# Low halves of the last three down chunks: a ScalarE negation and an accumulating transfer from GpSimd in place of a VectorE subtraction

## The chip, the cores and the metric

The kernel runs on one core of one Trainium2 chip. The metric is the device time of one execution in microseconds. Its engines are TensorE (PE, with weight loads as PEld), VectorE (DVE), ScalarE (ACT), GpSimd (POOL) and SyncE (SP), which issues most of the transfers. SBUF is the core's working memory.

## The reference

Two transformer blocks over 512 tokens of width 1024, in f32: a gated MLP layer with spatial mixing, a shared key/value projection with a dilated attention layer, and a second block of two attentions and a feed-forward layer. The change touches only the very end, the down projection of that feed-forward layer, with D_FF = 2816 = 22 x 128:

```python
h2 = _modulate(x, ln2_g[l], sh2, sc2)
y = (jax.nn.silu(h2 @ w_gate[l]) * (h2 @ w_up[l])) @ w_down[l]
x = x + g2[:, None, :] * y
```

## The kernel before

All weights stream through the core as 108 chunks of 128 rows, numbered w, in one fixed order. Every engine runs a program of its own, written out by hand, and they meet at semaphores.

To reach f32 accuracy, each chunk is split into two fp32r tiles: `w_hi` holds the rounded weights, `w_lo` the rest. The activations are split likewise, and each product is made of three matmuls: hi by hi, hi by lo, lo by hi. So a chunk passes through four steps:

- SP's `load` (L388) brings it from HBM to `w_raw[par]`, with par = w % 2. It waits until `lo_done` says that the low half of chunk w-2 is made, since that was the last reader of the raw buffer.
- ACT's `to_hi` (L575) copies `w_raw` to `w_hi`. It waits for the load and, by `mm_done`, for the matmuls of chunk w-2, which read the same `w_hi` and `w_lo`.
- DVE's `to_lo` (L1009) writes `w_lo = w_raw - w_hi` and counts `lo_done`.
- PE waits in `chunk_ready` (L1808) for `lo_done` and runs the matmuls (L1775).

There are two buffers of each tile, so chunk w is split while PE works on chunk w-1.

The down projection is done in two parts. The first 16 of the 22 row tiles (`FF1`) are handled earlier. The last six (`FF2`) come in chunks w = 104 to 107 (`W_DN2` to `W_END - 1`). Each of these has 6 x 256 = 1536 columns and gives two output tiles of 128 rows, 18 matmuls of 512 columns each, 36 in a chunk. Ahead of them come the gate and up chunks, up to w = 103. The split of chunk 104 is made inside that loop (`gate_up`, the call of `to_hi` and `to_lo` with `next_chunk`), so that only the chunks 105, 106 and 107 have their split in the code at the end. In program order, ACT's last gate work (`gu_hi`, L977) stands ahead of its `to_hi` of chunk 105.

After each output tile DVE's `update_x` (L1001) adds the gated result from PSUM to `x`, and SP sends that tile of `x` out (L507). These stores stand on SP's queue behind the four last loads. The PSUM tile that chunk w writes was freed by the `update_x` of chunk w-2.

Of the kernel before, what the change touches and what calls it, by code (L numbers as in the profile page):

```python
# [21 lines left out]
F32 = mybir.dt.float32  # L22
F32R = mybir.dt.float32r
ACT = mybir.ActivationFunctionType
# [16 lines left out]
FF1, FF2 = 16, 6  # L41
# [15 lines left out]
W_DN2 = W_GU2 + FF2  # L57
W_END = W_DN2 + 4
# [51 lines left out]
def program(nc, d):  # L110
# [4 lines left out]
    def at(name, shape, off, dt=F32):  # L115
        return nc.alloc_sbuf_tensor_at(name, shape, dt, offset=off)

    def take(nbytes, step=64):
        off = top[0]
        top[0] += (nbytes + step - 1) // step * step  # L120
        return off
# [10 lines left out]
    w_raw = [at(f"w_raw{s}", [P, 2048], take(8 * KB)) for s in range(2)]  # L132
# [13 lines left out]
    w_hi = [at(f"w_hi{s}", [P, 2048], off_whi[s], F32R) for s in range(2)]  # L146
    w_lo = [at(f"w_lo{s}", [P, 2048], off_wlo[s], F32R) for s in range(2)]
# [130 lines left out]
    def sem(name):  # L278
        return nc.alloc_semaphore(name)
# [4 lines left out]
    w_loaded = [sem("w_loaded0"), sem("w_loaded1")]  # L284
# [8 lines left out]
    hi_done, lo_done, lo_half_done = sem("hi_done"), sem("lo_done"), sem("lo_half_done")  # L293
# [24 lines left out]
    qk2_done, s2_freed, max2_part, exp2_done = sem("qk2_done"), sem("s2_freed"), sem("max2_part"), sem("exp2_done")  # L318
    inv2_done, p2_ready, turn2_done, pt2_done, pv2_done = sem("inv2_done"), sem("p2_ready"), sem("turn2_done"), sem("pt2_done"), sem("pv2_done")
    mhi_done, mlo_done, diff_freed = sem("mhi_done"), sem("mlo_done"), sem("diff_freed")  # L320
    tanhg_done, gz_done, guhi_done, gulo_done = sem("tanhg_done"), sem("gz_done"), sem("guhi_done"), sem("gulo_done")


# [16 lines left out]
    def ge(eng, semaphore, value):  # L340

        if not isinstance(value, int) or value > 0:
            eng.wait_ge(semaphore, value)
# [3 lines left out]
    def weights_at(u, par):  # L347

        if isinstance(u, int) and 2 * u + par in V_CHUNKS:
            return wv_hi[par], wv_lo[par]  # L350
        return w_hi[par], w_lo[par]
# [24 lines left out]
    with block:  # L376
# [3 lines left out]
        def _(sp):  # L380
            weights, ada_weights = d["weights"], d["ada"]

            def load(u, par, used=2048):

                src = weights[bass.ds(2 * u + par, 1), :, 0:used].rearrange("a p n -> p (a n)")
                sp.lower_ap_dma(src)
                ge(sp, lo_done, 2 * u + par - 3)
                sp.dma_start(w_raw[par][:, 0:used], src).then_inc(w_loaded[par], 16)  # L388
# [111 lines left out]
                for par in range(2):  # L500
                    load(u, par)
            for w in range(W_DN2, W_END):
                load(*divmod(w, 2), FF2 * 256)

            for m in range(KT):
                sp.wait_ge(acc_freed, 2 * W_DN2 - 15 + m)
# [4 lines left out]
        @block.gpsimd  # L511
        def _(pool):
            def stage(j, par):

                ge(pool, mix_done, j - 1)
                nc.gpsimd.tensor_tensor(v_stage[par][:, :, :], v[:, :, bass.ds(j * P, P)],
                                        v_stat[:, 5, :].unsqueeze(2).broadcast_to([P, TB, P]), ALU.mult).then_inc(v_staged, 1)

            def sum_squares(k, total, tile):

                for m in range(1, KT - 1):
                    pool.wait_ge(sq_ready, 8 * k + m + 1)
                    if m > 1:
                        pool.wait_ge(sq_added, 6 * k + m - 1)
                    nc.gpsimd.tensor_tensor(total, tile(0) if m == 1 else total, tile(m), ALU.add).then_inc(sq_added, 1)

            nc.gpsimd.memset(one_row[:, :], 1.0).then_inc(one_ready, 1)
            nc.gpsimd.memset(idle[:, :].bitcast(F32), 0.0).then_inc(idle_ready, 1)
            nc.gpsimd.memset(half_r[:, :].bitcast(F32), 0.0).then_inc(half_zeroed, 1)
            nc.gpsimd.memset(eps_tile[:, :], EPS)  # L530
            nc.gpsimd.memset(ones_r[:, :].bitcast(F32), 1.0).then_inc(ones_ready, 1)
            pool.wait_ge(half_zeroed, 1)
            pool.wait_ge(ones_ready, 1)
            for e in range(2):
                if e:
                    pool.wait_ge(half_ready, 1)
                part = slice(64 * e, 64 * e + 64)
                nc.gpsimd.memset(half_r[part, part].bitcast(F32), 1.0).then_inc(half_ready, 1)
            pool.wait_ge(half_ready, 2)
            pool.wait_ge(v_stat_dve, 3)  # L540
            stage(0, 0)
            stage(1, 1)
            with pool.Fori(1, AT // 2) as i:
                for par in range(2):
                    stage(2 * i + par, par)

            sum_squares(1, sq_sum[:, :], lambda m: sq_a[m % 2][:, :])

            def quarters(m):

                pool.wait_ge(exp_done, 4 * m + 4)
                ge(pool, spread_done, m)
                stats = row_stat[:, 0, :, :].rearrange("p k n -> p (k n)").unsqueeze(1).broadcast_to([P, 4, 16])
                nc.gpsimd.tensor_tensor(row_apart[:, :, :], stats, own_quarter.unsqueeze(2).broadcast_to([P, 4, 16]), ALU.mult).then_inc(apart_done, 1)

            pool.wait_ge(blocks_loaded, 16)
            for m in range(QH):
                quarters(m)
            pool.wait_ge(pv_done, 4 * QH)
            nc.gpsimd.memset(wf_hi[:, :, :].bitcast(F32), 0.0).then_inc(wf_zeroed, 1)  # L560
            nc.gpsimd.memset(wf_lo[:, :, :].bitcast(F32), 0.0).then_inc(wf_zeroed, 1)
            sum_squares(2, sq_sum[:, :], lambda m: sq[m % 2][:, :])
            sum_squares(3, sq_sum[:, :], lambda m: sq[m % 2][:, :])


        @block.scalar
        def _(act):
            eps_col = eps_tile[:, :]

            def to_hi(u, par, used=2048):  # L570

                act.wait_ge(w_loaded[par], 16 * u)
                if not (isinstance(u, int) and 2 * u + par == 2):
                    act.wait_ge(mm_done, 4 * u + 2 * par - 2)
                nc.scalar.activation(weights_at(u, par)[0][:, 0:used], w_raw[par][:, 0:used], ACT.Copy).then_inc(hi_done, 1)  # L575
# [411 lines left out]
            with act.Fori(W_GU2 // 2, W_DN2 // 2) as u:  # L987
                for par in range(2):
                    gate_up(u, 2 * (u - W_GU2 // 2) + par, par, FF1)

            for w in range(W_DN2 + 1, W_END):
                to_hi(*divmod(w, 2), FF2 * 256)


        @block.vector
        def _(dve):
            def f32(tile):
                return tile.bitcast(F32)
# [4 lines left out]
            def to_lo(u, par, used=2048):  # L1003

                dve.wait_ge(hi_done, 2 * u + par - 1)

                ge(dve, lo_done, 2 * u + par - 2)
                hi, lo = weights_at(u, par)
                nc.vector.tensor_tensor(lo[:, 0:used], w_raw[par][:, 0:used], f32(hi[:, 0:used]), ALU.subtract).then_inc(lo_done, 1)  # L1009
# [143 lines left out]
            def update_x(m, acc, gate, mm, n, dilate=False):  # L1153

                dve.wait_ge(mm_done, mm)
                xm = dilated(x[:, m, :]) if dilate else x[:, m, :]
                stt(xm, four(acc) if dilate else acc, mods[:, bass.ds(m + gate, 1)], xm, ALU.mult, ALU.add).then_inc(acc_freed, n)
# [357 lines left out]
            for c in range(4):  # L1515
                w = W_OUTB + c
# [190 lines left out]
            for c in range(4):  # L1707
                w = W_OUT2 + c
# [54 lines left out]
                    gate_up(u, 2 * (u - W_GU2 // 2) + par, par, FF1)  # L1763
            for c in range(4):
                w = W_DN2 + c
                if c < 3:
                    to_lo(*divmod(w + 1, 2), FF2 * 256)
                for half in range(2):
                    update_x(2 * c + half, G[2 * (w % 2) + half][:, :], GATE_2, 2 * w + half + 1, 1)

# [2 lines left out]
        def _(pe):  # L1773
# [34 lines left out]
            def chunk_ready(u, par):  # L1808
                pe.wait_ge(lo_done, 2 * u + par - 1)
# [157 lines left out]
            for c in range(NKV // 2):  # L1967
                w = W_KV + 2 * c
# [296 lines left out]
            for t in range(1, 5):  # L2265
# [3 lines left out]
                for u in range(12):  # L2269
# [15 lines left out]
                    if project:  # L2285
                        mi, w = u // 2, w0 + u // 4
# [75 lines left out]
            with pe.Fori(W_GU2 // 2, W_DN2 // 2) as u:  # L2362
                gate_up(u)
            for w in range(W_DN2, W_END):
                chunk_ready(*divmod(w, 2))
                for half in range(2):
                    pe.wait_ge(acc_freed, 2 * w + half - 19)
                for piece in (range(FF2 - 2), range(FF2 - 2, FF2)) if w == W_DN2 else (range(FF2),):
                    if w == W_DN2:

                        pe.wait_ge(gulo_done, FF1 + piece[-1] + 1)
                    for half in range(2):
                        last = columns(G[2 * (w % 2) + half][:, :], w % 2, half, FF2, gu_hi, gu_lo_of, piece)
                        if piece[-1] == FF2 - 1:
                            last.then_inc(mm_done, 1)
# [89 lines left out]
```

## Time and profile before

| | |
|---|---|
| time, median of 3 runs (lowest, highest) | 1402.61 us (1402.58, 1405.28) |
| time of the profiled execution | 1403.06 us |
| its span in the profile | 1401.0 us |
| PE busy | 1387.4 us, 99% |
| DVE busy | 963.5 us, 69% |
| ACT busy | 646.1 us, 46% |
| POOL busy | 50.9 us, 4% |
| granted TensorE clock over the span | 1.0 of full speed |

The span is what the profiler saw between the first and the last instruction. The time of the execution is 2.06 us longer. PE's busy time includes the drain of pipelined matmuls, so that its share does not say how near its peak it is; the starts of its instructions do. Chunks 104 to 107 fill about the last 36 us.

### The profile page before, as it was taken

Reading aid. Unit: us, or ns where it says so; the run is one execution under the profiler, and the core shown is the slowest. Engines: PE = TensorE matmul, PEld = TensorE weight load, DVE = VectorE, ACT = ScalarE, POOL = GpSimd, SP = SyncE. Lnnn points to the kernel's source line nnn. Section 1 sums busy time; section 2 is a strip of 40 time slices with the busy share of each in tenths; the row PEclk is TensorE's granted clock in tenths of the full one; section 3 lists DMA queues with packets and bytes.
Section 4 is the critical chain, followed back from the end, with each engine's and each line's share of the span. In section 5 each row is a group of like instructions: output and inputs, shape, how many; then the busy total and the mean of one; then the engine's idle time right before and its main releaser. Section 6 shows DMA issues by size and latency. Waiting matters only on the chain.

```text
span 1401.0 us, 19731 instructions
## 1 busy us (share of the span) xinstructions
PE 1387.4 (99%) x7274; PEld 1158.0 (83%) x7274; DVE 963.5 (69%) x1573; ACT 646.1 (46%) x1046; POOL 50.9 (4%) x55
## 2 busy tenths in 40 slices
PE   8999999999999999999999999999999999999999
PEld 6998888888888888888888777777788888888887
DVE  6976777777898688888887777778775433332333
ACT  4744222333366566666654656666644222211221
POOL 0001000001100000000002000000020000000000
PEclk9999999999999999999999999999999999999999
DMA  9994554457723211112212221111122222222222
GB/s 374 376 394 182 180 179 176 178 203 284 304 76 124 82 69 61 61 61 66 84 60 91 82 100 61 61 61 61 61 91 90 90 102 108 90 90 101 103 74 83
DMA packets 35329, 181.23 MB, mean 129 GB/s; under 512 B 4153, under 2 KB 4921, under 8 KB 20930
## 3 DMA queue, kind: packets, MB, share of 16 engines
q1 hardware_dynamic: 34050, 177.95, 34.5%
q10 hardware_dynamic: 1216, 2.44, 0.5%
q8 instruction: 39, 0.64, 0.2%
q14 instruction: 24, 0.20, 0.0%
HBM read 177.74 MB, written 2.11 MB: 128 GB/s over the span
## 4 chain that ended last, share of the span: by engine, by line
PE 89%; DVE 6%; ACT 2%; DMA 1%; issue 1%; SPq 0%; ACTq 0%; DVEq 0%
PE acc L1775 80%; PE ada L1775 3%; PE norm L1775 2%; PE turn L1775 2%; DMA ada_up<-in_ada_first 1%; PE turn L2069 1%; PE turn L2212 1%; DVE hx L1001 1%; DVE w_lo L1009 1%; DVE s L1574 0%; DVE hk_lo L1001 0%; DVE h_lo L1001 0%; DVE v L1638 0%; ACT hk_hi L599 0%; DVE c_masked L1580 0%
## 5 line engine op out<-in xcount | busy, mean ns | idle before, releaser
L1775 PE MATMUL acc<-h_hi,w_hi 128*128 128x512 f32 x984 | 390.1, 396 | 0.0
L1775 PE MATMUL acc<-h_hi,w_lo 128*128 128x512 f32 x984 | 384.3, 391 | 0.0
L1775 PE MATMUL acc<-h_lo,w_hi 128*128 128x512 f32 x984 | 383.6, 390 | 0.0
L1009 DVE TENSOR_TENSOR w_lo<-w_raw,w_hi 128x2048 fp32r<-128x2048 f32 (+1 forms) x92 | 212.8, 2313 | 58.7 <-ACT w_hi L575 58.6
L575 ACT ACTIVATE w_hi<-w_raw 128x2048 fp32r<-128x2048 f32 (+1 forms) x93 | 176.0, 1892 | 111.4 <-PE acc L1775 111.3
L1775 PEld LDWEIGHTS acc<-h_hi,w_lo 128*128 128x128 f32 x984 | 184.8, 188 | 39.4
L1775 PEld LDWEIGHTS acc<-h_hi,w_hi 128*128 128x128 f32 x984 | 185.2, 188 | 38.2 <-issue 1.2
L1775 PEld LDWEIGHTS acc<-h_lo,w_hi 128*128 128x128 f32 x984 | 185.1, 188 | 36.7
L1775 PE MATMUL acc<-wv_hi,h_hi 128*128 128x256 f32 x320 | 89.6, 281 | 0.0
L1001 DVE SCALAR_TENSOR_TENSOR x<-acc,mods,x 128x512 f32<-128x512 f32 (+1 forms) x40 | 32.9, 827 | 81.6 <-PE acc L1775 81.6
L1775 PE MATMUL acc<-wv_lo,h_hi 128*128 128x256 f32 x320 | 88.2, 277 | 0.0
L1775 PE MATMUL acc<-wv_hi,h_lo 128*128 128x256 f32 x320 | 87.5, 277 | 0.0
L581 ACT ACTIVATE y<-norm,eps_tile 128x512 f32<-128x512 f32 x54 | 37.2, 689 | 77.2 <-PE norm L1775 75.7
L1001 DVE SCALAR_TENSOR_TENSOR gu<-tanh_g,acc 128x512 f32<-128x512 f32 x21 | 14.4, 688 | 82.5 <-PE acc L1775 82.4
L1775 PE MATMUL acc<-gu_lo,w_hi 128*128 128x512 f32 x176 | 68.5, 389 | 0.0
L1775 PE MATMUL acc<-gu_hi,w_hi 128*128 128x512 f32 x176 | 68.5, 389 | 0.0
L1775 PE MATMUL acc<-gu_hi,w_lo 128*128 128x512 f32 x176 | 68.5, 389 | 0.0
L977 ACT ACTIVATE gu_hi<-gu 128x512 f32 (+1 forms) x22 | 13.9, 632 | 117.2 <-DVE gu L1001 117.2
L1775 PEld LDWEIGHTS acc<-wv_hi,h_hi 128*128 128x128 f32 x320 | 60.2, 188 | 1.2 <-issue 1.0
L1775 PEld LDWEIGHTS acc<-wv_lo,h_hi 128*128 128x128 f32 x320 | 60.1, 188 | 0.2
L1775 PEld LDWEIGHTS acc<-wv_hi,h_lo 128*128 128x128 f32 x320 | 59.6, 188 | 0.0
L1001 DVE SCALAR_TENSOR_TENSOR ada_out<-ada_out,csil 128x1024 f32<-128x1024 f32 x32 | 38.4, 1224 | 17.3 <-DMA ada_out<-in_ada 17.0
(306 smaller groups left out, 2528.2 us busy)
## 6 DMA issues: line engine op xcount, KB each, us to landing
w_raw<-in_weights SPq DMA_DIRECT2D x102, 1024.0 KB, 4.8
ada_v<-in_ada SPq DMA_DIRECT2D x32, 512.0 KB, 6.3
ada_raw<-in_ada SPq DMA_DIRECT2D x32, 512.0 KB, 5.8
ada_out<-in_ada SPq DMA_DIRECT2D x32, 512.0 KB, 6.3
ada_up<-in_ada_first SPq DMA_DIRECT2D x8, 1024.0 KB, 17.3
w_raw<-in_weights SPq DMA_DIRECT2D x4, 768.0 KB, 4.1
x<-in_x SPq DMA_DIRECT2D x2, 1024.0 KB, 6.0
w_first<-in_weights SPq DMA_DIRECT2D x4, 512.0 KB, 13.7
```

The source lines that it names most:

```text
L575: nc.scalar.activation(weights_at(u, par)[0][:, 0:used], w_raw[par][:, 0:used], ACT.Copy).then_inc(hi_done, 1)
L581: nc.scalar.activation(y0[:, :], total, ACT.Ln, scale=1.0 / count, bias=eps_col).then_inc(ln_done, 1)
L977: nc.scalar.activation(gu_hi[:, f, :], gu[par][:, :], ACT.Copy).then_inc(guhi_done, 1)
L1001: return nc.vector.scalar_tensor_tensor(out, in0, scalar, in1, op0, op1, **more)
L1009: nc.vector.tensor_tensor(lo[:, 0:used], w_raw[par][:, 0:used], f32(hi[:, 0:used]), ALU.subtract).then_inc(lo_done, 1)
L1775: return nc.tensor.matmul(out, lhsT, rhs, start=start, stop=stop)
L2069: turned = nc.tensor.transpose((T0, T1)[c % 2][:, P * b:P * b + P], s_b[tile][:, lo:lo + P], ident)
L2212: turned = nc.tensor.transpose(T0[:, P * b:P * b + P], s_2[n % 3][:, 0, P * b:P * b + P], ident)
```

## The change

For the chunks 105, 106 and 107, DVE no longer makes `w_lo`. Instead

- ACT, right after `to_hi`, waits for its own result (`hi_done`) and writes `w_lo = -w_hi` with a second activation, counting `neg_done`;
- GpSimd waits for `neg_done` and issues a transfer from `w_raw` to `w_lo` with `accum_op=add`: for each element the transfer adds what it read from `w_raw` to what stands in `w_lo`. Its end is counted by `rest_added[par]`;
- PE waits for `rest_added` instead of `lo_done` ahead of the chunks 105 to 107;
- SP's load of chunk 107 overwrites the raw buffer of chunk 105, so it waits for `rest_added[1]` of chunk 105 instead of `lo_done`.

The values computed are the same. GpSimd issues no transfer anywhere in the kernel before.

```diff
--- before.py
+++ after.py
@@ -318,6 +318,7 @@
     qk2_done, s2_freed, max2_part, exp2_done = sem("qk2_done"), sem("s2_freed"), sem("max2_part"), sem("exp2_done")
     inv2_done, p2_ready, turn2_done, pt2_done, pv2_done = sem("inv2_done"), sem("p2_ready"), sem("turn2_done"), sem("pt2_done"), sem("pv2_done")
     mhi_done, mlo_done, diff_freed = sem("mhi_done"), sem("mlo_done"), sem("diff_freed")
+    neg_done, rest_added = sem("neg_done"), [sem("rest_added0"), sem("rest_added1")]
     tanhg_done, gz_done, guhi_done, gulo_done = sem("tanhg_done"), sem("gz_done"), sem("guhi_done"), sem("gulo_done")
 
 
@@ -500,7 +501,10 @@
                 for par in range(2):
                     load(u, par)
             for w in range(W_DN2, W_END):
-                load(*divmod(w, 2), FF2 * 256)
+                if w < W_END - 1:
+                    load(*divmod(w, 2), FF2 * 256)
+            sp.wait_ge(rest_added[1], 16)
+            sp.dma_start(w_raw[1][:, 0:FF2 * 256], weights[W_END - 1][:, 0:FF2 * 256]).then_inc(w_loaded[1], 16)
 
             for m in range(KT):
                 sp.wait_ge(acc_freed, 2 * W_DN2 - 15 + m)
@@ -561,6 +565,11 @@
             nc.gpsimd.memset(wf_lo[:, :, :].bitcast(F32), 0.0).then_inc(wf_zeroed, 1)
             sum_squares(2, sq_sum[:, :], lambda m: sq[m % 2][:, :])
             sum_squares(3, sq_sum[:, :], lambda m: sq[m % 2][:, :])
+
+            used = FF2 * 256
+            for w in range(W_DN2 + 1, W_END):
+                pool.wait_ge(neg_done, w - W_DN2)
+                pool.dma_start(w_lo[w % 2][:, 0:used].bitcast(F32), w_raw[w % 2][:, 0:used], accum_op=ALU.add).then_inc(rest_added[w % 2], 16)
 
 
         @block.scalar
@@ -988,8 +997,11 @@
                 for par in range(2):
                     gate_up(u, 2 * (u - W_GU2 // 2) + par, par, FF1)
 
+            used = FF2 * 256
             for w in range(W_DN2 + 1, W_END):
-                to_hi(*divmod(w, 2), FF2 * 256)
+                to_hi(*divmod(w, 2), used)
+                act.wait_ge(hi_done, w - 1)
+                nc.scalar.activation(w_lo[w % 2][:, 0:used], w_hi[w % 2][:, 0:used].bitcast(F32), ACT.Copy, scale=-1.0).then_inc(neg_done, 1)
 
 
         @block.vector
@@ -1763,8 +1775,6 @@
                     gate_up(u, 2 * (u - W_GU2 // 2) + par, par, FF1)
             for c in range(4):
                 w = W_DN2 + c
-                if c < 3:
-                    to_lo(*divmod(w + 1, 2), FF2 * 256)
                 for half in range(2):
                     update_x(2 * c + half, G[2 * (w % 2) + half][:, :], GATE_2, 2 * w + half + 1, 1)
 
@@ -2362,7 +2372,10 @@
             with pe.Fori(W_GU2 // 2, W_DN2 // 2) as u:
                 gate_up(u)
             for w in range(W_DN2, W_END):
-                chunk_ready(*divmod(w, 2))
+                if w == W_DN2:
+                    chunk_ready(*divmod(w, 2))
+                else:
+                    pe.wait_ge(rest_added[w % 2], 32 if w == W_END - 1 else 16)
                 for half in range(2):
                     pe.wait_ge(acc_freed, 2 * w + half - 19)
                 for piece in (range(FF2 - 2), range(FF2 - 2, FF2)) if w == W_DN2 else (range(FF2),):
```

The end of ACT's program, after the last gate work; `w_hi_62` and `w_lo_64` are the tiles of the odd chunks (105, 107), `w_hi_61` and `w_lo_63` those of chunk 106. Before:

```order
L987 REGISTER_ALU
L987 COMPARE_AND_BRANCH
L575 ACTIVATE w_hi_62<-w_raw_53 128x1536 [waits mm_done,w_loaded1]
L575 ACTIVATE w_hi_61<-w_raw_52 128x1536 [waits mm_done,w_loaded0]
L575 ACTIVATE w_hi_62<-w_raw_53 128x1536 [waits mm_done,w_loaded1]
L376 UNCONDITIONAL_BRANCH
```

And now:

```order
L996 REGISTER_ALU
L996 COMPARE_AND_BRANCH
L584 ACTIVATE w_hi_62<-w_raw_53 128x1536 [waits mm_done,w_loaded1]
L1004 ACTIVATE w_lo_64<-w_hi_62 128x1536 [waits hi_done]
L584 ACTIVATE w_hi_61<-w_raw_52 128x1536 [waits mm_done,w_loaded0]
L1004 ACTIVATE w_lo_63<-w_hi_61 128x1536 [waits hi_done]
L584 ACTIVATE w_hi_62<-w_raw_53 128x1536 [waits mm_done,w_loaded1]
L1004 ACTIVATE w_lo_64<-w_hi_62 128x1536 [waits hi_done]
L377 UNCONDITIONAL_BRANCH
```

Behind each copy to `w_hi` stands a second activation of the same size, which waits for the copy ahead of it.

The end of SP's queue: the loads of the chunks 104 to 107 and the stores. Before:

```order
L388 DMA w_raw_52<-in_weights 128x1536 [waits lo_done]
L388 DMA w_raw_53<-in_weights 128x1536 [waits lo_done]
L388 DMA w_raw_52<-in_weights 128x1536 [waits lo_done]
L388 DMA w_raw_53<-in_weights 128x1536 [waits lo_done]
L507 DMA out<-x 128x512 [waits acc_freed] x8
L376 UNCONDITIONAL_BRANCH [waits stored]
```

And now:

```order
L389 DMA w_raw_52<-in_weights 128x1536 [waits lo_done]
L389 DMA w_raw_53<-in_weights 128x1536 [waits lo_done]
L389 DMA w_raw_52<-in_weights 128x1536 [waits lo_done]
L507 DMA w_raw_53<-in_weights 128x1536 [waits rest_added1]
L511 DMA out<-x 128x512 [waits acc_freed] x8
L377 UNCONDITIONAL_BRANCH [waits stored]
```

The order is the same; the fourth load, with the eight stores behind it, waits for a transfer from GpSimd to land instead of for VectorE.

The end of GpSimd's program. Before:

```order
L525 TENSOR_TENSOR sq_sum<-sq_sum,sq_94 128x512 [waits sq_added,sq_ready]
L525 TENSOR_TENSOR sq_sum<-sq_sum,sq_93 128x512 [waits sq_added,sq_ready]
L525 TENSOR_TENSOR sq_sum<-sq_sum,sq_94 128x512 [waits sq_added,sq_ready]
L525 TENSOR_TENSOR sq_sum<-sq_sum,sq_93 128x512 [waits sq_added,sq_ready]
L376 UNCONDITIONAL_BRANCH
```

And now:

```order
L529 TENSOR_TENSOR sq_sum<-sq_sum,sq_94 128x512 [waits sq_added,sq_ready]
L529 TENSOR_TENSOR sq_sum<-sq_sum,sq_93 128x512 [waits sq_added,sq_ready]
L572 DMA w_lo_64<-w_raw_53 128x1536 [waits neg_done]
L572 DMA w_lo_63<-w_raw_52 128x1536 [waits neg_done]
L572 DMA w_lo_64<-w_raw_53 128x1536 [waits neg_done]
L377 UNCONDITIONAL_BRANCH
```

Three accumulating transfers have come in behind GpSimd's last additions, in the order of the chunks 105, 106, 107.

## Rows read from the trace of the kernel before

**Rows 1.** The page, busy time and share of TensorE.

```profile
PE 1387.4 (99%) x7274; PEld 1158.0 (83%) x7274; DVE 963.5 (69%) x1573; ACT 646.1 (46%) x1046; POOL 50.9 (4%) x55
```

**Rows 2.** Chain that ended last, from 1340 us: start, duration, what.

```profile
1339.99 57.81 PE acc L1775 x255
...
1397.82 0.75 DVE x L1001
```

**Rows 3.** Timeline of TensorE around the first matmul of chunk 105.

```profile
1372.92 0.39 PE L1775 MATMUL acc<-gu_hi,w_lo 128*128 128x512 f32 x1
1373.14 0.39 PE L1775 MATMUL acc<-gu_hi,w_hi 128*128 128x512 f32 x1
```

**Rows 4.** Busy time by stage: chunks 105, 106 and 107.

```profile
core 0: us, PE busy (x) PEld busy (x) DVE busy (x) ACT busy (x) POOL busy (x), PEclk, DMA share, GB/s
1373.14:1381.30 8.16, 8.16 (x37) 6.76 (x36) 3.26 (x3) 1.49 (x1) 0.00 (x0) 1.00 0.28 103
1381.30:1389.46 8.16, 8.16 (x37) 6.76 (x36) 3.26 (x3) 1.49 (x1) 0.00 (x0) 1.00 0.17 64
1389.46:1397.62 8.16, 8.16 (x37) 6.57 (x35) 1.50 (x2) 0.00 (x0) 0.00 (x0) 1.00 0.17 64
```

**Rows 5.** Timeline of ScalarE: copies to w_hi of chunks 105, 106, 107.

```profile
1366.64 1.47 ACT L575 ACTIVATE w_hi<-w_raw 128x1536 fp32r<-128x1536 f32 x1
...
1373.40 1.49 ACT L575 ACTIVATE w_hi<-w_raw 128x1536 fp32r<-128x1536 f32 x1 [5.29 <-PE acc L1775]
...
1381.56 1.49 ACT L575 ACTIVATE w_hi<-w_raw 128x1536 fp32r<-128x1536 f32 x1 [6.67 <-PE acc L1775]
```

**Rows 6.** Timeline of VectorE: subtractions of chunks 105 to 107, and updates of x.

```profile
1368.15 1.76 DVE L1009 TENSOR_TENSOR w_lo<-w_raw,w_hi 128x1536 fp32r<-128x1536 f32 x1 [0.55 <-ACT w_hi L575]
...
1373.35 0.75 DVE L1001 SCALAR_TENSOR_TENSOR x<-acc,mods,x 128x512 f32<-128x512 f32 x1 [0.61 <-PE acc L1775]
1374.92 1.76 DVE L1009 TENSOR_TENSOR w_lo<-w_raw,w_hi 128x1536 fp32r<-128x1536 f32 x1 [0.83 <-ACT w_hi L575]
...
1383.08 1.76 DVE L1009 TENSOR_TENSOR w_lo<-w_raw,w_hi 128x1536 fp32r<-128x1536 f32 x1 [0.83 <-ACT w_hi L575]
...
1397.82 0.75 DVE L1001 SCALAR_TENSOR_TENSOR x<-acc,mods,x 128x512 f32<-128x512 f32 x1 [3.33 <-PE acc L1775]
```

**Rows 7.** Timeline of SyncE's queue: load of chunk 107, the stores.

```profile
1369.93 0.33 SPq L388 DMA_DIRECT2D w_raw<-in_weights  x1
...
1372.76 26.17 SPq L507 DMA_DIRECT2D out<-x  x8
```

**Rows 8.** Transfers: size each, median us from issue to landing.

```profile
w_raw<-in_weights SPq DMA_DIRECT2D x102, 1024.0 KB, 4.8
...
w_raw<-in_weights SPq DMA_DIRECT2D x4, 768.0 KB, 4.1
...
out<-x SPq DMA_DIRECT2D x8, 256.0 KB, 2.0
...
v_b<-v_turn SPq DMA_DIRECT2D x16, 32.0 KB, 2.5
```

**Rows 9.** GpSimd by line: its commonest instructions, mean ns of one.

```profile
L525 POOL TENSOR_TENSOR sq_sum<-sq_sum,sq 128x512 f32<-128x512 f32 x10 | 17.7, 1774 | 27.2 <-ACT sq L615 26.6
L516 POOL TENSOR_TENSOR v_stage<-v,v_stat 128x512 f32<-128x512 f32 x16 | 16.6, 1041 | 259.8 <-PE turn L1775 146.0 <-DVE v_stat L1001 113.9
```

**Rows 10.** Timeline of TensorE at the start of the kernel.

```profile
5.94 2.93 PE L1775 MATMUL ada<-idle 128*128 128x512 f32 x6
...
8.24 0.63 PE L1775 MATMUL ada<-idle 128*128 128x512 f32 x1
```

**Rows 11.** Busy time by stage at the start; the clock is near the end.

```profile
5.94:8.87 2.93, 2.93 (x8) 2.17 (x8) 0.81 (x2) 2.82 (x6) 0.00 (x0) 1.00 1.03 425
```

## Prediction

> **What bounds the kernel now.** The page's busy times come first: TensorE is busy for 99% of the span [rows 1]. The chain that ended last, read for the final stretch, is one unbroken piece of TensorE of 57.81 us, up to 1397.80, and then one VectorE update of 0.75 us [rows 2]. So at the end only TensorE's pace counts, and another engine counts only where it makes TensorE wait. The first matmul of chunk 105 starts at 1373.14 [rows 3]; the three stages from there are 8.16 us long each, filled wholly by TensorE [rows 4]: chunk 105 from 1373.14, 106 from 1381.30, 107 from 1389.46, its last matmul near 1397.7. In the three stages VectorE is busy for 3.26, 3.26 and 1.50 us, with the same 8.16 us for TensorE. Taking work from VectorE therefore gives nothing by itself. What must be read is how early each low half is ready.
>
> **The change part by part.** Its deadline for chunk 105 is 1373.14. Today ScalarE copies from 1366.64 and VectorE subtracts from 1368.15 for 1.76 us, so the low half is there at 1369.91 [rows 5, 6], 3.23 us early. For chunk 106 ScalarE can only start at 1373.40, when the matmuls of chunk 104 have released the tiles; the low half is there at 1374.92 + 1.76 = 1376.68, 4.62 us ahead of 1381.30. For chunk 107 it is the same 8.16 us later.
>
> *Removed:* three subtractions of 1.76 us. They lie beside matmuls, and the updates of x behind them wait for TensorE anyway: gain 0. VectorE's last update [rows 6] starts right after the last matmul and is unchanged.
>
> *Added on ScalarE:* three activations of 128x1536. The nearest row is the copy of the same shape, 1.49 us [rows 5]. It can start when the subtraction starts today, since it waits for the same thing: 1368.15. It ends at 1369.64 for chunk 105. Nothing is held up behind it: ScalarE idles 5.29 and 6.67 us ahead of its next copies [rows 5].
>
> *Added, the transfer.* Call X the time from the end of the negation to the landing of the accumulating transfer. For chunk 105 TensorE waits D1 = 1369.64 + X - 1373.14 = X - 3.50. Everything later on TensorE moves by D1. Chunk 106: its negation starts at 1374.92 and ends at 1376.41, its transfer lands at 1376.41 + X, and TensorE comes to it at 1381.30 + D1 = 1377.80 + X. It is early by 1.39 us whatever X is: the first stall pays for the second chunk. Chunk 107: ScalarE starts when chunk 105 is done, at 1381.56 + D1; the negation starts 1.52 us later (1383.08 - 1381.56, rows 5 and 6) and takes 1.49, so it ends at 1384.57 + D1, and the transfer lands at 1384.57 + D1 + X. TensorE comes to it at 1389.46 + D1. It waits D2 = X - 4.89. The sum is D1 + D2 = 2X - 8.39 where X is above 4.89, X - 3.50 between 3.50 and 4.89, and nothing below.
>
> So all depends on X, which this trace does not show: nothing here accumulates, and GpSimd issues no transfer. **From below:** the plain load of the same 768 KB takes 4.1 us to land, one of 1024 KB takes 4.8, hence 0.7 us for each 256 KB and 2.0 us fixed; a 256 KB store takes 2.0 us in all [rows 8], which with twice 0.7 for the other 512 KB gives 3.4 us for 768 KB that are read from SBUF. That is the lower end, and it costs nothing. **From above:** if the reading of the source, the reading of the destination and the writing did not overlap, three times 4.1 = 12.3 us. **Between them** I build it up: 2.0 fixed, 3 x 0.7 = 2.1 for the source, 2.1 more because the destination must be read through the same engines too, 6.2 in all; and for GpSimd, whose cost of issuing one no row has, about one of its instructions, 1.04 to 1.77 us [rows 9], mean 1.4. I take X = 7.6, nearer to the plain loads than to the upper end, since those rows are the same bytes on the same engines.
>
> A page of the Trainium skill can be held against this: "DMA: Bandwidth & Descriptors", section "Anatomy of one DMA — SWDGE (gpsimd) path", gives a transfer issued by GpSimd a fixed 2.0 us and its bytes at 436 GB/s, which is 3.8 us for 768 KB, and by that D1 would be 0.3 us and the change free. The rows of the loads agree on the fixed part (2.0) but are for one read. "Collectives: The Full Stack", section "The bandwidth ceiling: the fold count and why AG ≠ RS ≠ AR", says that a reducing transfer reads two sources through one ring and runs at half the rate; by both pages together it would be 2.0 + 3.6 = 5.6 us and the sum 2.8. No run here shows either yet.
>
> With X = 7.6: D1 = 4.10, D2 = 2.71, together 6.81 us.
>
> *Moved on SP's queue:* the load of chunk 107 now starts at 1369.64 + 7.6 = 1377.2 instead of 1369.93 [rows 7], and lands at 1381.3; ScalarE wants it only at 1385.7. Cover 4.4 us; without it each us late would be a us on D2. Behind it on SP stand the eight stores, the first two of which go out at 1377 instead of 1372.76; the last ones follow their updates as before. So the cost here is 0, but traffic meets: the transfer of chunk 106 (1376.4 to 1384.0) shares the engines with this load and two stores. If that made it later by all their 2.1 + 0.7 + 0.7 = 3.5 us, chunk 106 would be late by 2.1 us, yet chunk 107's landing does not depend on it and is 2.71 us after TensorE's arrival, so the delay is swallowed there. The transfer of chunk 107 shares with about two 256 KB stores, one for each output tile; half of their 1.4 us, 0.7, I add.
>
> *Sum:* 6.81 + 0.7 = 7.5 us. Against the profiled execution: 1403.06 + 7.5 = 1410.6. The median of the runs shown is 0.45 us below that execution, so 1402.61 + 7.5 = 1410.1.
>
> **The rivals.** About 0.2%, or 2.8 us, is what a measurement can tell from no change here.
>
> (a) *The transfer is hidden or nearly so, and the time stays.* It decides at 2X - 8.39 = 2.8, so at X = 5.6. For it speaks the plain load of 4.1 us: with that, D1 = 0.6 and the time is 1403.2. Against it: the second read, and an issuer that no row prices. 15%.
>
> (b) *The three passes of the transfer do not overlap, or the adder in it is slow.* X = 12.3 gives 2 x 12.3 - 8.39 = 16.2, with the stores 16.9, so 1419.5. The sharing with the load would be longer too. No row speaks for or against. 13%.
>
> (c) *TensorE comes out of its waits at its lower clock.* The start of the kernel shows matmuls of 128x512 0.46 us apart, five from 5.94 to 8.24 [rows 10], about twice the 0.227 us (8.16 / 36) of the last stages, though the granted clock in that stretch reads 1.00 [rows 11], so the trace's clock does not settle which level of 1.2 and 2.4 GHz it was. How many would run so after D1 no row says; the six of rows 10 would cost 6 x 0.23 = 1.4 us, a whole chunk 36 x 0.23 = 8.3. I take 14, which is 3.3 us more: 1413.4. The Trainium skill, "TensorE: Matmul & The Clock Gate", section "What's actually happening", says that an idle array falls to half its clock and must be busy for a while to get it back; no row here shows that in mid-kernel. 12%.
>
> (d) *Faster.* Nothing waits for VectorE at the end, and the matmuls keep 8.16 us in a stage with 3.26 us of VectorE and in one with 1.50 [rows 4]. Even if all its traffic had slowed TensorE it would have to win 2.8 us out of 24.5. 2%.
>
> **How the numbers follow.** The forecast (X between 5.6 and about 10.5, so 1405.4 to 1416) has 58%, (a) 15%, (b) 13%, (c) 12%, (d) 2%. Slower by over 0.2%: 58 + 13 + 12 = 83%. Within: 15%. Faster: 2%. The range leaves out the lower part of (a), all of (d) and the upper end of (b): 1403.4 to 1419.0.
>
> **What would show each step.** In the changed kernel's timeline TensorE should be idle ahead of chunk 105 by about 4.1 us and ahead of 107 by 2.7 to 3.4, each released by a transfer to w_lo, and not ahead of 106. The negation should take 1.49 us and start at 1368.15. The table of transfers should give three of 768 KB from GpSimd with 6 to 8 us to landing. The matmuls should stay 0.227 us apart; 0.46 would be (c). I would be wrong if X is under 5.6 or over 10.5, if chunk 106 stalls and the two others don't take it up, or if something outside the last 35 us moves.

## The result, and the profile after

The changed kernel takes 1409.20 us in the median of 6 runs (1408.36 to 1410.19), before took 1402.67 (6 runs). The ratio is 1.0044, 95% interval 1.0031 to 1.0057: slower, as forecast, by 0.44%. Ratios here and below are estimated from all executions together and differ a little from the quotient of the two medians. The profiled execution took 1408.36 us, with a span of 1406.5. Of the 18 executions of before that ran beside E1 to E4, one took 1975.95 us at a granted clock of 0.656, a slow state, and is left out of every figure.

The page of the changed kernel answers to [rows 1]; below it come the new queue, the group of matmuls that now has idle time ahead of it (busy us, mean ns, idle before), and the new transfers (KB each, median us from issue to landing):

```profile
PE 1387.8 (99%) x7274; PEld 1156.9 (82%) x7274; DVE 958.7 (68%) x1570; ACT 650.6 (46%) x1049; POOL 53.6 (4%) x58
...
q0 software_dynamic: 432, 2.36, 0.8%
...
L1785 PE MATMUL acc<-gu_hi,w_hi 128*128 128x512 f32 x176 | 68.7, 390 | 5.0 <-DMA w_lo<-w_raw 5.0
...
w_lo<-w_raw POOLq DMA_DIRECT2D x3, 768.0 KB, 5.8
```

TensorE's busy time is the same (1387.8 against 1387.4) while the span is 5.5 us longer, and 5.0 us of idle time stand ahead of one group, released by the transfer to `w_lo`. The rest of the kernel did not move: ScalarE's copy for chunk 105 starts at 1366.57, before at 1366.64 [rows 5].

Timeline of TensorE in the changed kernel, at the start of chunk 105 and of chunk 106 (answers to [rows 3]):

```profile
1372.84 0.39 PE L1785 MATMUL acc<-gu_hi,w_lo 128*128 128x512 f32 x1
1375.75 0.50 PE L1785 MATMUL acc<-gu_hi,w_hi 128*128 128x512 f32 x1 [2.52 <-DMA w_lo<-w_raw]
1376.09 0.40 PE L1785 MATMUL acc<-gu_lo,w_hi 128*128 128x512 f32 x1
...
1383.82 0.39 PE L1785 MATMUL acc<-gu_hi,w_lo 128*128 128x512 f32 x1
1386.67 0.50 PE L1785 MATMUL acc<-gu_hi,w_hi 128*128 128x512 f32 x1 [2.47 <-DMA w_lo<-w_raw]
```

The matmul at 1372.84 would have been followed at 1373.07; chunk 105 begins at 1375.75, 2.68 us late. Chunk 106 should follow 1383.82 at 1384.05 and begins at 1386.67, 2.62 us late. Nothing is ahead of chunk 107. The first matmul after each wait is followed after 0.34 us instead of 0.227, and the first update of chunk 105 comes 4.41 us after the chunk's start instead of 4.28, so each restart costs 0.13. Together 2.68 + 2.62 + 2 x 0.13 = 5.56.

ScalarE's copies and negations for the chunks 105 and 106, all three issues on GpSimd, and VectorE's updates (the first one of chunk 105 and the last of all), answers to [rows 5, 6]:

```profile
1366.57 1.47 ACT L584 ACTIVATE w_hi<-w_raw 128x1536 fp32r<-128x1536 f32 x1
1368.07 1.49 ACT L1004 ACTIVATE w_lo<-w_hi 128x1536 fp32r<-128x1536 f32 x1
1373.33 1.48 ACT L584 ACTIVATE w_hi<-w_raw 128x1536 fp32r<-128x1536 f32 x1 [3.77 <-PE acc L1785]
1374.84 1.49 ACT L1004 ACTIVATE w_lo<-w_hi 128x1536 fp32r<-128x1536 f32 x1
```

```profile
1369.88 1.01 POOL L572 DMA_DIRECT2D w_lo<-w_raw  x1 [338.72 <-ACT w_lo L1004]
1376.64 0.86 POOL L572 DMA_DIRECT2D w_lo<-w_raw  x1 [5.75 <-ACT w_lo L1004]
1387.59 0.85 POOL L572 DMA_DIRECT2D w_lo<-w_raw  x1 [10.09 <-ACT w_lo L1004]
```

```profile
1380.16 0.75 DVE L1013 SCALAR_TENSOR_TENSOR x<-acc,mods,x 128x512 f32<-128x512 f32 x1 [6.14 <-PE acc L1785]
...
1403.33 0.75 DVE L1013 SCALAR_TENSOR_TENSOR x<-acc,mods,x 128x512 f32<-128x512 f32 x1 [3.33 <-PE acc L1785]
```

From ScalarE's copy for chunk 105 to the start of the last update there are now 1403.33 - 1366.57 = 36.76 us; before there were 1397.82 - 1366.64 = 31.18 [rows 5, 6]. This stretch, 5.58 us longer, is the measure used below. A whole execution of any of these kernels, before among them, may take 2 to 3 us more or less from what happens in its first 105 us (the same copy of a chunk starts at 102.46 us in some traces, at 104.65 in others), and the stretch leaves that out.

Transfers to `w_lo` in the changed kernel, min/median/max from issue to landing, then SyncE's queue (answers to [rows 7]) and the end of the chain:

```profile
DMA to landing us min/median/max: 5.8/5.8/10.0
```

```profile
1375.72 0.33 SPq L507 DMA_DIRECT2D w_raw<-in_weights  x1
1376.10 28.34 SPq L511 DMA_DIRECT2D out<-x  x8
```

```profile
1376.64 9.99 DMA w_lo<-w_raw
1386.63 0.04 issue
1386.67 16.63 PE acc L1785 x72
...
1403.33 0.75 DVE x L1013
```

Two of the three transfers land 5.8 us after issue, the one of chunk 106 takes 10.0 and is now a link of the chain that ended last. What kept it is in the table of queues, first from 1378 to 1381, then from 1381 to 1385 (packets, MB, share of the 16 engines; q1 is SyncE's queue, q0 GpSimd's):

```profile
q1 hardware_dynamic: 317, 0.95, 98.9%
q0 software_dynamic: 1, 0.01, 1.0%
```

```profile
q0 software_dynamic: 130, 0.76, 93.3%
q1 hardware_dynamic: 95, 0.16, 10.7%
```

GpSimd issued at 1376.64; the data of its first transfer began to flow some 1.5 us after its issue (1371.4 against 1369.88), so these should have begun at 1378. In the first three microseconds in which its data could have flowed, the engines worked on SyncE's queue for 98.9% of their time: the load of chunk 107, issued at 1375.72, and the two stores behind it. One packet of GpSimd's came through. Then it had the engines nearly to itself.

### The profile page after: what moved, and what is told of

It reads as the page before. It is cut to its first block, busy times and chain, and to the rows that moved or that the text cites. A ratio compares the mean times of both kernels' runs of the same rounds, so it can differ in the third digit from the quotient of the medians.

```text
span 1406.5 us, 19731 instructions
## 1 busy us (share of the span) xinstructions
PE 1387.8 (99%) x7274; PEld 1156.9 (82%) x7274; DVE 958.7 (68%) x1570; ACT 650.6 (46%) x1049; POOL 53.6 (4%) x58
## 4 chain that ended last, share of the span: by engine, by line
PE 82%; DVE 8%; DMA 5%; ACT 2%; issue 2%; SPq 1%; ACTq 0%; DVEq 0%
PE acc L1785 73%; DMA ada_out<-in_ada 3%; PE ada L1785 3%; DVE w_lo L1021 2%; PE norm L1785 2%; PE turn L1785 2%; DMA ada_up<-in_ada_first 1%; PE turn L2079 1%; PE turn L2222 1%; DVE hx L1013 1%; DMA w_lo<-w_raw 1%; DVE s L1586 0%; DVE h_lo L1013 0%; DVE hk_lo L1013 0%; DVE ada_out L1013 0%
## 5 line engine op out<-in xcount | busy, mean ns | idle before, releaser
L1021 DVE TENSOR_TENSOR w_lo<-w_raw,w_hi 128x2048 fp32r<-128x2048 f32 x89 | 207.6, 2332 | 56.4 <-ACT w_hi L584 56.3
```

## The experiments

In all of them TensorE's other matmuls are 0.227 us apart at the full clock. "Before" is the kernel before, run on the same chip.

**E1, a buffer of its own for the load of chunk 107.** The load is issued right behind that of chunk 106 and waits for nobody; ScalarE and GpSimd read the new buffer for chunk 107 (their lines are left out here).

```diff
+    raw_last = at("raw_last", [P, FF2 * 256], big + 16 * KB)
...
-            sp.wait_ge(rest_added[1], 16)
-            sp.dma_start(w_raw[1][:, 0:FF2 * 256], weights[W_END - 1][:, 0:FF2 * 256]).then_inc(w_loaded[1], 16)
+            sp.dma_start(raw_last[:, :], weights[W_END - 1][:, 0:FF2 * 256]).then_inc(last_loaded, 16)
```

> Chunk 107 is loaded into a buffer of its own, right behind the load of chunk 106, so that its load runs long before the transfers. Theory S (the transfer of chunk 106 took 10.0 us because the load of chunk 107 ran beside it): it takes 5.8 to 6.5 us here, TensorE does not wait ahead of chunk 106, and waits about 1.2 us ahead of chunk 107 (6.1 us from the end of the negation to the landing, less 4.89). Total over before 2.7 + 1.2 + twice 0.13 for restarting = 4.2 us, 1406.8. Rival T (it is the stores, or the even buffer or the second transfer is slow by itself): still 9 to 10 us and 2.5 us of wait ahead of 106; time as the changed kernel, 1408.4 to 1409.2.

Its timeline of TensorE has two waits, and its transfers land so:

```profile
1378.75 0.50 PE L1791 MATMUL acc<-gu_hi,w_hi 128*128 128x512 f32 x1 [2.56 <-DMA w_lo<-w_raw]
...
1396.39 0.50 PE L1791 MATMUL acc<-gu_hi,w_hi 128*128 128x512 f32 x1 [1.02 <-DMA w_lo<-raw_last]
```

```profile
DMA to landing us min/median/max: 5.7/5.9/6.4
```

The stretch is 1404.90 - 1369.53 = 35.37, 4.19 over before. The transfer of 106 takes 6.4 us, no wait is left ahead of chunk 106, and one of 1.02 us has come up ahead of 107, as theory S had it. But this edit moves the stores as well. They no longer stand behind the load, go out at 1375.64 and 1377.01, and their data are through by 1379.6, when the transfer of 106 is issued. So E1 takes the load and both stores out of its way, and does not tell which of them held it. The whole time, 1409.92 us against 1404.34 (ratio 1.0040, 1.0027 to 1.0053), is 3 us above the figure expected. The profiled execution is the one of 1409.92, and there the copy for chunk 105 starts 2.89 us later than in the trace of before (1369.53 against 1366.64), so the excess lies ahead of the stretch. The other four executions read a mean granted clock of 0.999.

**E2, the stores held until the transfer of chunk 106 has landed.** One line more:

```diff
+            sp.wait_ge(rest_added[0], 16)
             for m in range(KT):
                 sp.wait_ge(acc_freed, 2 * W_DN2 - 15 + m)
```

> The stores of x wait until the transfer of chunk 106 has landed; the load of chunk 107 still runs beside it. Theory S (the load does it): the transfer of chunk 106 takes 8 to 9.5 us, since 768 KB of load remain beside it and about 512 KB of stores are gone; wait ahead of 106 1 to 2 us. Rival T1 (the stores do it): 6 to 7 us, no wait ahead of 106, 1.2 us ahead of 107. The end of the kernel is not changed, since only the first stores are held.

The transfer took 7.0 us, less than theory S said and the figure of its rival. Where nothing of SyncE's stands ahead of it (E1, and E10 below) it takes 6.4, next to the load alone 7.0, next to the load and two stores 10.0. In packets: its data, due at 1381.3, begin at 1382.1, 0.8 late, and in the changed kernel they begin 3.0 late. So the load alone is not the culprit; it is what the queue ahead of GpSimd's transfer adds up to, and the two stores are the larger part. Two stores without the load were not tried. There was no wait ahead of 106 and one of 1.00 ahead of 107, and yet the stretch was 1406.63 - 1369.73 = 36.90, 5.72 over before (time 1409.73, ratio 1.0038, 1.0025 to 1.0051). The missing time is in TensorE's timeline behind its first wait:

```profile
1378.93 0.60 PE L1786 MATMUL acc<-gu_hi,w_hi 128*128 128x512 f32 x1 [2.53 <-DMA w_lo<-w_raw]
1379.33 0.63 PE L1786 MATMUL acc<-gu_lo,w_hi 128*128 128x512 f32 x1
1379.76 0.63 PE L1786 MATMUL acc<-gu_hi,w_lo 128*128 128x512 f32 x1
...
1382.68 0.40 PE L1786 MATMUL acc<-gu_hi,w_hi 128*128 128x512 f32 x1
1382.91 0.39 PE L1786 MATMUL acc<-gu_lo,w_hi 128*128 128x512 f32 x1
```

```profile
core 0: us, PE busy (x) PEld busy (x) DVE busy (x) ACT busy (x) POOL busy (x), PEclk, DMA share, GB/s
1378.90:1382.30 3.40, 3.37 (x8) 2.60 (x9) 0.00 (x0) 0.59 (x1) 0.86 (x1) 0.54 0.74 237
1382.60:1384.90 2.30, 2.30 (x11) 1.90 (x11) 0.00 (x0) 0.00 (x0) 0.00 (x0) 1.00 1.04 214
```

After 2.53 us of waiting, matmuls come 0.427 us apart, eight of them, 1.6 us more than at full pace, and the granted clock of that stretch is 0.54, then 1.00 again: the lower of the two levels, 1.2 GHz.

**E3, only chunk 105 by transfer**, 106 and 107 by VectorE as before. **E4, only chunk 106.** In both the negation and the transfer stand under a condition, and VectorE's subtraction is back for the others:

```diff
+                if w == W_DN2 + 1:        # E4: + 2
                     pool.wait_ge(neg_done, 1)
...
+                if c < 3 and c + 1 != 1:  # E4: != 2
+                    dve.wait_ge(hi_done, w)
+                    k = (w + 1) % 2
+                    nc.vector.tensor_tensor(w_lo[k][:, 0:FF2 * 256], w_raw[k][:, 0:FF2 * 256], f32(w_hi[k][:, 0:FF2 * 256]), ALU.subtract).then_inc(lo_done, 1)
```

> Only chunk 105 is made by negation and transfer; 106 and 107 go back to VectorE. Both theories: TensorE waits 2.7 us ahead of chunk 105, nothing ahead of 106 and 107 (the late load of 107 is covered), so 2.8 us over before: 1405.5. If the delay of the first transfer were worth less than its wait, the total would be smaller.

> Only chunk 106 is made by negation and transfer; 105 and 107 go back to VectorE, and the load of chunk 107 starts at 1369.9 as before, so it has landed before the transfer starts. Theory S: the transfer takes 5.8 to 6.5 us, TensorE waits 1.2 to 1.8 us ahead of chunk 106, total 1.3 to 1.9 us over before: 1404.0 to 1404.6. Rival T2 (the even buffer or that place in time is slow, load or not): 10 us, wait 5.3, 1408.

E3: the only wait is that of 2.51 us (2.67 by the starts), the stretch 1403.10 - 1369.12 = 33.98, 2.80 over before. E4: the transfer took 5.9 us, with this wait:

```profile
1383.78 0.50 PE L1791 MATMUL acc<-gu_hi,w_hi 128*128 128x512 f32 x1 [1.22 <-DMA w_lo<-w_raw]
```

The stretch is 1400.45 - 1367.74 = 32.71, 1.53 over before (time 1405.58 against 1404.34, ratio 1.0011, 1.0002 to 1.0020). So the even buffer is as fast as the odd one, and each chunk by itself costs what its slack leaves over. In E4 the load of chunk 107 waits for `lo_done` again, starts at 1371.03 and is over before the transfer. A store met the transfer instead: SyncE issued it at 1379.30, when GpSimd's data were just about to flow. The table of queues from 1379 to 1383, and the time of that store, which takes 2.0 us in the median before [rows 8]:

```profile
q0 software_dynamic: 128, 0.79, 98.8%
```

```profile
out<-x SPq DMA_DIRECT2D x1, 256.0 KB, 5.1
```

Here SyncE's store is the later one, and in those 4 us not one packet of its queue (q1) came through.

E3 shows the clock in its runs: the three executions with a mean granted clock of 1.000 took 1405.4 to 1408.2 us, the four with 0.999 took 1409.7 to 1410.4; its ratio, 1.0033 (1.0021 to 1.0046), is above the 2.8 us of its stretch in part for that reason, and in part because the start of the kernel differs between executions.

**E5, the changed kernel again, and E6, the same with its waits filled.** E6 puts matmuls ahead of the waits before the chunks 105 and 106:

```diff
+                if w in (W_DN2 + 1, W_DN2 + 2):
+                    for _ in range(11):
+                        mm(AD[:, :], gu_lo[:, 0, 0:P], gu_hi[:, 0, :], True, True)
```

> The changed kernel itself, unchanged, on the chip of the next ones. Theory C (the two waits of 2.5 us sometimes bring TensorE out at the lower clock, at 1.6 us each time, which is where the spread of 1408.4 to 1410.2 comes from): again 5.5 us over before at best and 6 to 7.5 us in the middle, with a spread of some 2 us that before does not have.

> Eleven matmuls of gu tiles into an unused PSUM bank stand ahead of TensorE's waits before chunk 105 and 106; their result is not read. They fill 2.5 us of each wait and end before the transfer lands. Theory C: TensorE is never idle long enough to lose its clock, so the time is the best of the changed kernel, 5.3 to 5.6 us over before, its middle about 0.5 to 1 us below that of the changed kernel on this chip, every matmul 0.227 us apart. Rival (the spread comes from the transfers or the start of the kernel): same median as the changed kernel.

E5: 1412.19 us against 1405.49 (ratio 1.0049, 1.0036 to 1.0063), 6.7 us in the median; all five executions have a mean granted clock of 0.999. Its trace has a lowered clock in chunk 105, and this wait ahead of 106:

```profile
1376.09 0.50 PE L1785 MATMUL acc<-gu_hi,w_hi 128*128 128x512 f32 x1 [2.53 <-DMA w_lo<-w_raw]
...
1386.76 0.50 PE L1785 MATMUL acc<-gu_hi,w_hi 128*128 128x512 f32 x1 [0.62 <-DMA w_lo<-w_raw]
```

The first update of chunk 105 comes 6.00 us after 1376.09 instead of 4.41, but the wait ahead of chunk 106 is 0.62 us instead of 2.47: the transfer lands when it lands, and swallows the loss. The stretch is 36.91, 5.73 over before, so 1.6 us of lost clock behind the first wait cost 0.15 against the 5.58 of the first trace. (Chunk 107 starts 0.24 us late here.) E6, around chunk 105:

```profile
1373.56 2.65 PE L1785 MATMUL ada<-gu_hi,gu_lo 128*128 128x512 f32 x11
1376.24 0.50 PE L1785 MATMUL acc<-gu_hi,w_hi 128*128 128x512 f32 x1
1376.58 0.39 PE L1785 MATMUL acc<-gu_lo,w_hi 128*128 128x512 f32 x1
```

The eleven take the wait, chunk 105 goes on at 1376.24 at full pace, and all seven executions read 1.000. Its median is 3.8 us over before (1409.29, ratio 1.0036, 1.0024 to 1.0047), but the intervals of E5 and E6 overlap, and E6's own stretch is 36.98, 5.80 over before (its transfer of 106 took 10.2 us). The 3.8 is mostly a matter of how the executions fell in the two groups that the start of the kernel makes: E6 at 1408.1 to 1409.3 (four of seven) and 1411.5 to 1412.2, before at 1402.9 to 1403.7 (three of 17) and 1405.1 to 1406.2. Between the medians of the lower groups lie 5.5 us, between those of the upper ones 6.2; for E5 the upper ones are 6.8 apart. So the filling keeps the clock; that it makes the changed kernel faster is not settled, since behind the first wait the second one absorbs most of the loss.

**E7, own buffer and halves.** E1, with negation and transfer in two pieces of 768 columns:

```diff
+                for e in range(2):
+                    part = slice(768 * e, 768 * e + 768)
+                    pool.wait_ge(neg_done, 2 * (w - W_DN2) - 1 + e)
+                    pool.dma_start(w_lo[w % 2][:, part].bitcast(F32), (raw_last if w == W_END - 1 else w_raw[w % 2])[:, part], accum_op=ALU.add).then_inc(rest_added[w % 2], 16)
```

> Chunk 107 is loaded into its own buffer, and negation and transfer are done in two halves of 768 columns, so that the first half's transfer is issued 0.7 us earlier. The transfer's data phase of 3.7 to 4 us fills all 16 engines, so halving saves only the earlier start: waits of 2.0 us ahead of 105, none ahead of 106, 0.5 ahead of 107, total 2.5 to 3 us over before. If what counts were the time from issue to landing of one transfer, with 2 us fixed, two halves would be no faster than one: 4.2 us over before, as with the own buffer alone.

A miss: 1411.38 us against 1405.49 (ratio 1.0035, 1.0021 to 1.0049). TensorE waited 2.26 us ahead of 105 and 1.41 ahead of 107, where E1 has 2.56 and 1.02, and lost its clock behind the first for eight matmuls; the stretch is 37.05, 5.87 over before. Without the 1.6 us of clock that is 4.3, the 4.2 of the rival. The halves land 3.9 to 6.0 us after their issues, and the second issue stands behind the first on GpSimd (together 1.74 to 1.90 us). The earlier start gained 0.30 us ahead of 105 and lost 0.39 ahead of 107. That the second issue and its landing took the gain back is read from these rows, not tested apart.

**E8, a plain copy from GpSimd. E9, a plain copy from ScalarE's queue.** E8 drops `accum_op`, so `w_lo` holds `w_raw` and the low half is wrong; E9 leaves the addition out too and moves the issue:

```diff
-                pool.dma_start(w_lo[w % 2][:, 0:used].bitcast(F32), w_raw[w % 2][:, 0:used], accum_op=ALU.add).then_inc(rest_added[w % 2], 16)
+                act.wait_ge(neg_done, w - W_DN2)
+                act.dma_start(w_lo[w % 2][:, 0:used].bitcast(F32), w_raw[w % 2][:, 0:used]).then_inc(rest_added[w % 2], 16)
```

> The same three transfers from GpSimd without the addition, a plain copy of w_raw to w_lo, so that the low half is wrong by w_hi; all else as in the changed kernel. Theory R (the second read costs 1.9 us of the engines): data phase 1.9 us instead of 3.7 to 4, issue to landing 3.9 us for the first, TensorE waits 0.6 to 0.8 us ahead of 105, and the transfer of 106 takes 2 us less. Total 1 to 3 us over before. Rival (the time is set by GpSimd's issue and the row packets, not by bytes): 5.8 us again, as the changed kernel.

> As the plain copy from GpSimd (the low half is then w_raw, without the subtraction), but each copy is issued by ScalarE behind its negation. Theory R (the bytes cost the same whoever issues; GpSimd's issue and start cost about 1 us more): 2.5 to 3.3 us from issue to landing for the first instead of 3.7, no wait ahead of chunk 105, the transfer of 106 shorter than 6.6 us; total 0.5 to 1.5 us over before. Rival (start and landing are the same for both issuers): 3.7 us, and 2.2 us over before.

The transfers of E8, then of E9, min/median/max:

```profile
DMA to landing us min/median/max: 3.5/3.7/6.6
```

```profile
DMA to landing us min/median/max: 3.5/3.6/5.3
```

Issuing from ScalarE saves 0.1 us of 3.7. The queue of the transfer of chunk 105, first with the addition (the changed kernel, 1371 to 1375.3), then without (E8, 1374 to 1376.4):

```profile
q0 software_dynamic: 135, 0.79, 92.1%
```

```profile
q0 software_dynamic: 144, 0.79, 80.2%
```

With the addition the 16 engines are full for 92.1% of 4.3 us = 4.0 us, without for 80.2% of 2.4 = 1.9. So the addition doubles the engines' time for the same 0.79 MB and costs 2.1 us, which is the whole of 5.8 - 3.7. That the second half is the read of the destination fits the factor of two; the rows do not name it. Theory R holds on the cost of the addition and fails on the issuer. The stretches are 33.38 (2.20 over before) and 31.77 (0.59), the times 1407.64 against 1405.49 (ratio 1.0013, 1.0004 to 1.0022) and 1406.13 against 1403.19 (1.0021, 1.0010 to 1.0032). The difference between the stretches is the transfer of 106, 6.6 us in E8 and 5.3 in E9, and the 0.3 us between the end of the negation and the issue on GpSimd.

**E10, the load of chunk 107 behind the transfer of chunk 106.** One more wait ahead of the load:

```diff
             sp.wait_ge(rest_added[1], 16)
+            sp.wait_ge(rest_added[0], 16)
```

> The load of chunk 107 waits for the transfer of chunk 106 as well. Theory Q (work that SyncE's queue has already given to the engines goes ahead of GpSimd's transfer, so the transfer of 106 stood 2.6 us behind the load and two stores): now the transfer of 106 takes 5.8 to 7 us (the stores are held back behind the load too) and TensorE does not wait ahead of 106; but the load of 107 lands near 1386.8 instead of before 1384.3, so the chain of 107 is 2.5 us later and TensorE waits 3.5 us there: the stall moves, total 6 to 6.7 us over before, with the clock lost there at times for 1.6 more.

The transfer of 106 took 6.4 us and chunk 106 had no wait, as theory Q said. The timeline of TensorE, at the chunks 105 and 107:

```profile
1379.25 0.50 PE L1786 MATMUL acc<-gu_hi,w_hi 128*128 128x512 f32 x1 [2.53 <-DMA w_lo<-w_raw]
...
1380.52 0.45 PE L1786 MATMUL acc<-gu_hi,w_lo 128*128 128x512 f32 x1
1380.77 0.63 PE L1786 MATMUL acc<-gu_hi,w_hi 128*128 128x512 f32 x1
1381.19 0.63 PE L1786 MATMUL acc<-gu_lo,w_hi 128*128 128x512 f32 x1
...
1400.78 0.50 PE L1786 MATMUL acc<-gu_hi,w_hi 128*128 128x512 f32 x1 [3.27 <-DMA w_lo<-w_raw]
1401.12 0.56 PE L1786 MATMUL acc<-gu_lo,w_hi 128*128 128x512 f32 x1
1401.47 0.63 PE L1786 MATMUL acc<-gu_hi,w_lo 128*128 128x512 f32 x1
```

From 1380.1 to 1386.5 the table of queues has the 144 packets of this transfer, one of the instruction queue and none of SyncE's, so the 6.4 us are not a store's doing, here or in E1; why they are not 5.8 is open. The wait has moved to chunk 107, 3.27 us, and the clock fell behind both waits. The load of 107 took 5.2 us (median 4.1 before, [rows 8]), and all of chunk 107 hangs on it, so the wait there absorbed the clock lost behind the first. Nothing absorbs it behind the second. The stretch is 1410.90 - 1370.06 = 40.84, 9.66 over before, more than the 6 to 6.7 with 1.6 for the clock that were expected; the time 1414.76 against 1403.19 (ratio 1.0076, 1.0061 to 1.0091).

**E11, own buffer, waits filled.** E1 with eleven filling matmuls ahead of 105 and four ahead of 107.

> Own buffer for the load of chunk 107, and unused matmuls that fill TensorE's waits, eleven ahead of chunk 105 and four ahead of 107. With the sharing gone and the clock kept, what is left is twice the transfer's own length beyond its slack: 2.6 + 1.2 + restarting, 4.0 to 4.3 us over before in the stretch from ScalarE's copy of chunk 105 to the last update of x, and a granted clock of 1.000 in every execution.

The stretch is 1402.37 - 1366.98 = 35.39, 4.21 over before; the median 1407.34 against 1403.19, 4.15 over (ratio 1.0029, 1.0018 to 1.0040). All seven executions read 1.000. Here median and stretch agree. It is the best version with accumulating transfers in all three chunks, and still slower than before, where no wait exists to be shortened.

## Why the prediction was right, and where it was not

**What bounds the kernel: right.** Only TensorE's waits at the end moved. The three subtractions gave nothing, and the negation takes 1.49 us at 1368.07, as read from the copy.

**The first wait: right in kind, 1.4 us too long.** D1 was put at 4.10 and measured 2.68. X, from the end of the negation at 1369.56 to the landing at 1375.7, is 6.1 instead of 7.6. The term that was mis-sized is GpSimd's, 1.4 us, which came from the length of its arithmetic: the issue comes 0.3 us after the negation, and then costs 0.1 over ScalarE's (E8, E9). The rest was near: 2.0 + 2.1 = 4.1 for one read measured 3.7 (E8), and 2.1 for the second measured 2.1. The Trainium skill's "Collectives: The Full Stack", section "The bandwidth ceiling: the fold count and why AG ≠ RS ≠ AR", has a reducing transfer at half the rate because of its second read: 4.0 against 1.9 us of full engines agree. "DMA: Bandwidth & Descriptors", section "Anatomy of one DMA — SWDGE (gpsimd) path", gives 3.8 us for the plain copy, and E8 agrees with 3.7. Rival (a), which had the 4.1 us of a plain load for it, fell by the 2.1 us of the addition.

**"It is early by 1.39 us whatever X is": wrong.** This is the step that failed. It holds only while X is the same for every transfer, and the transfer of chunk 106 took 10.0 us. I had seen the meeting with the load and two stores and bounded it by 3.5 us of their own traffic; it was 4.2, and with it the wait ahead of 106 is 2.62. I also wrote that chunk 107 would swallow such a delay, since it had 2.71 us of its own to wait; it had 1.2. My own sign of being wrong, that chunk 106 stalls and the others do not take it up, came true. The first 3.0 are spent behind SyncE's queue, and a further store at 1385 meets its end. Taking load and stores out of the way brings 6.4 us and no wait (E1), as does putting them later (E10); holding the stores alone brings 7.0 and no wait (E2).

**D2 ahead of chunk 107: 0 instead of 2.71.** By the formula 107 would wait X - 4.89 = 1.2 with the measured X; the wait ahead of 106 gave it the time. Where 106 does not wait, it appears, 1.02 in E1 and 1.00 in E2. The 0.7 us for stores beside that transfer was nothing either: 5.8 us.

**The sum: near by two errors that partly cancel, which is luck.** Forecast were 4.10 + 2.71 + 0.7 = 7.5; the trace has 2.68 + 2.62 + 0.26 = 5.56, where 0.26 is the restarting, a term that I did not have. The formula at the measured X gives 2 x 6.1 - 8.39 = 3.8, and the 106 sharing turns it to 5.6.

**Rival (c), the lower clock: real, in most executions.** It is not in the profiled execution, but E2, E5, E7 and E10 show it, 8 matmuls at 0.427 instead of the 14 at 0.46 that I took: 1.6 us. The changed kernel reads 0.999 in 4 of its first 6 executions and in 5 of 5 of E5; with the waits filled it is 1.000 in 14 of 14. That the median lies 6.5 us over before while the profiled execution is 5.3 over its own fits this only in part: behind the first wait the loss is swallowed (E5), behind the second no trace of the changed kernel shows one, and one of the two executions that read 1.000 took 1410.19. E6 did not settle it, as said. The Trainium skill, "TensorE: Matmul & The Clock Gate", section "What's actually happening", has an idle array fall to half clock, and these traces agree.

## What to carry to other kernels

An accumulating transfer in SBUF took twice the engines' time of a plain copy: here 4.0 us of full engines and 5.8 us to landing for 768 KB, against 1.76 us for the VectorE instruction that it replaces, so it belongs only where its deadline is that far off. Before giving a transfer a cost, list what the other queues will have issued ahead of it at that moment, for the move itself may have delayed those (here the load of chunk 107 and the stores behind it) into its way. And where a new wait of a few microseconds on TensorE can't be avoided, price the clock behind it as well, unless another wait follows that absorbs it.

## What the runs showed of the hardware

GpSimd's transfer got one packet in the 3 us in which SyncE's queue had work (98.9% of the engines' time), though both rows are shares of the same 16 engines. It is not that SyncE's queue goes first: in E4 GpSimd's data had begun, and a store of SyncE's got no packet in 4 us (98.8%) and landed after 5.1 us instead of 2.0. In both cases the transfer that had come first went on nearly alone. "DMA: Bandwidth & Descriptors" in the Trainium skill, section "Queues, rings and completion order", has each engine take turns between the queues packet by packet; these stretches of the traces do not look so, and the measurement decides. What holds the later transfer back, whether the order inside the engines or the way its work reaches them, is open.

The clock did not always fall right behind a wait: in E10 TensorE had waited 2.53 us, then ran six matmuls from 1379.25 at full pace, and only from 1380.77 on are they 0.42 us apart.
